# Output projection of a first block as three rounded products of high and low parts, with the loads of two expert halves moved

## The chip, the core and the metric

The kernel runs on one core of one Trainium2 chip. The metric is the time of one execution in device microseconds (us). Engines are named as in the profile: PE (TensorE, matrix products), PEld (its weight loads), DVE (VectorE), ACT (ScalarE), POOL (GpSimd) and SP (SyncE, which only issues loads here). PSUM is the memory that PE writes, in eight banks; the rest of the data lies in SBUF.

## What is computed

Two transformer blocks follow each other on 256 tokens of 1024 features. The change lies in the first, at the last line of its mixer and just ahead of its experts:

```python
def hybrid_mixer(h, ...):
    ...                                   # projections, mLSTM in 4 heads -> y_m, trailing means -> y_p
    return jnp.concatenate([y_m, y_p], axis=-1) @ w_out      # (256 x 1024) @ (1024 x 1024)

def first_block(x, ...):
    h = rmsnorm(x, norm1_g[l])
    x = x + hybrid_mixer(h, ...)
    h = rmsnorm(x, norm2_g[l])
    x = x + moe_ffn(h, ...)               # 32 experts, the best 4 of each token, three 1024 x 1024 matrices each
    return rmsnorm(x, normf_g)
```

The first 512 features of `y` are the heads' (`y_m`), the last 512 the pooled groups' (`y_p`). All is in float32. The second block, with two attention branches and a feed-forward part, comes behind and isn't touched.

## The kernel before

**Phases.** `phase_a` computes the first mixer, its normalisation and the router; `phase_b` runs the 32 experts one after the other; `phase_c`, `phase_e` and `phase_d` are the second block. Each engine has its own program in each phase, written out in order, and semaphores connect them. Nothing is reordered by a scheduler.

**Two ways to multiply.** PE can take float32 operands as they are, or as a rounded type (float32r). For the projections of the first mixer (`Splits`) the weights come in units of 128 by 1024. ACT copies a unit into the rounded type (the high part, L263), and DVE or POOL subtracts that from the original (the low part, L266). A unit is multiplied in three passes: high by high, activation's low by weight's high, activation's high by weight's low (L1142 to L1149 and L1164 to L1171). There are three buffers each for high and low parts, `high_first` and `low_first`; unit u lies in buffer u modulo 3. The high and low parts of the activations are `hTh_first` and `hTl_first`. The last four units, 16 to 19, are those of the output gate.

**The output projection** takes float32 as it is. PE runs `pooled_half(n, t)` (L1239) for column half n and row half t over the four pooled feature chunks, and after the transposes of the gated heads (L1251) it adds the four chunks of the heads (L1263). There are 32 products of 128 by 512; the trace has two records for each. `yT` holds the transposed activations, in the first half of `spare[0]`.

**What PE waits for there.** POOL computes the trailing means in a chain (L889 to L893), and PE multiplies them by `pool_w` (L1226) into two banks. ACT scales them into `yT` (L821). DVE meanwhile divides numerators by denominators (L1000 to L1010), normalises and gates the heads (L1020, L1024), and evicts their transposes (L1028). After the last product of each half DVE adds it to `x` (L1038), ACT squares, and the normalisation goes on row half by row half.

**Loads.** w_out lies in two pieces of `ring25`, OUT0 and OUT1. An expert has six halves of 2 MB: half n of all is number n mod 6 of expert n div 6, in the order gate, gate, up, up, down, down. Eleven are loaded in `phase_a`: 0 to 7 into the eight regular places, and 47, 71 and 95 (`Pieces.LATE`) into `spare[0]`, `spare[1]` and `last_spare`. The rest follow in `phase_b`, each as soon as PE has used the half whose place it takes (L604). `spare[1]` shares memory with `hTh_first`, `last_spare` with `high_first` and `low_first`. The three tables of biases (`btab`, L766) must be there before expert 0 begins. SP issues all of these in a fixed order and stands at each wait.

## Time and profile before

| | us |
|---|---|
| median of 3 runs | 1648.52 (1648.29 to 1649.60) |
| the profiled execution | 1648.02 |
| its span on the core | 1646.3 |
| PE busy | 1624.4 (99%) |
| DVE, ACT, POOL busy | 613.7, 475.8, 302.4 |
| PE waits for POOL's trailing means, ahead of 82.46 | 1.38 |
| output projection on PE, float32 products | 84.58 to 113.2 |
| expert 0 begins | 129.66 |
| experts end | 1036 |

All times in the text are counted from the start of the span. A row of a timeline may merge several like instructions, whose number stands behind the x; its duration then runs from the first start to the last end. Matrix products overlap a little, so the distance of two starts is the better measure of their cost than their length. In brackets stands the idle time of the engine ahead of the row and what ended it.

### The profile page before, as it was taken

To read this page: it belongs to the slowest core of one execution; us is meant where nothing else is said; L and a number is where in the kernel's file an instruction comes from. 1 tells how busy PE (TensorE), PEld (TensorE's weight loads), DVE (VectorE), ACT (ScalarE), POOL (GpSimd) and SP (SyncE) were. 2 spreads that over 40 slices of the span, in tenths; PEclk is the share of its full clock that TensorE was granted. 3 is DMA by queue.
4 is the path that set the end of the run, shared out by engine and by line. 5 is a ranking of instruction groups with operands and counts; after the bars stand their busy time and mean duration, and the time that the engine had idled before them with its cause. 6 is when DMAs were issued, how large, how long until landed. Compare 5 with 4: busy or idle time off the path is not lost. (4 is left out here: it accounts for less than half of the span.)

```text
span 1646.3 us, 22758 instructions
## 1 busy us (share of the span) xinstructions
PE 1624.4 (99%) x9272; PEld 946.4 (57%) x9272; DVE 613.7 (37%) x1144; ACT 475.8 (29%) x695; POOL 302.4 (18%) x192
## 2 busy tenths in 40 slices
PE   9999999999999999999999999999999999999998
PEld 8843333333333333333333333698998999999986
DVE  7743212112121212121121211675485244468852
ACT  5421110111111111111011111574555454454443
POOL 3500000000000000000000000535333624445552
PEclk9999999999999999999999999999999999999999
DMA  9698999999999999999999999353133215456552
GB/s 350 221 367 338 428 427 426 428 427 426 428 426 427 429 426 427 426 428 428 428 428 428 428 428 422 125 179 128 53 123 134 103 52 195 166 166 203 167 192 102
DMA packets 92919, 507.67 MB, mean 308 GB/s; under 512 B 8987, under 2 KB 32584, under 8 KB 68264
## 3 DMA queue, kind: packets, MB, share of 16 engines
q1 hardware_dynamic: 92696, 506.00, 76.1%
q8 instruction: 61, 1.00, 0.3%
q10 hardware_dynamic: 144, 0.52, 0.1%
q14 instruction: 18, 0.15, 0.0%
HBM read 505.46 MB, written 1.05 MB: 308 GB/s over the span
## 5 line engine op out<-in xcount | busy, mean ns | idle before, releaser
L186 POOL TENSOR_TENSOR low<-ring,high 128x1024 fp32r<-128x1024 f32 x81 | 199.6, 2465 | 1262.8 <-ACT high L183 1262.7
L1593 PE MATMUL ps<-ring,x 128*64 128x512 f32 x1536 | 337.5, 594 | 1.8 <-DMA ring<-in_w_up 1.8
L1593 PEld LDWEIGHTS ps<-ring,x 128*64 128x64 f32 x1536 | 108.0, 137 | 227.5 <-issue 222.4
L183 ACT CAST high<-ring 128x1024 fp32r<-128x1024 f32 x162 | 168.2, 1047 | 201.4 <-PE ps L1727 125.5
L1720 PE MATMUL ps<-hTh,high 128*128 128x256 f32 x800 | 198.8, 285 | 2.4 <-DVE hTl L633 1.9
L1721 PE MATMUL ps<-hTl,high 128*128 128x256 f32 x800 | 197.6, 284 | 0.0
L1626 PE MATMUL ps<-ring,x 128*64 128x512 f32 x752 | 171.7, 598 | 0.0
L186 DVE TENSOR_TENSOR low<-ring,high 128x1024 fp32r<-128x1024 f32 x81 | 111.1, 1371 | 146.7 <-ACT high L183 146.6
L1720 PEld LDWEIGHTS ps<-hTh,high 128*128 128x128 f32 x800 | 153.9, 192 | 4.2 <-issue 3.8
L1721 PEld LDWEIGHTS ps<-hTl,high 128*128 128x128 f32 x800 | 154.0, 192 | 0.0
L1466 DVE TENSOR_SCALAR hT<-ps 128x512 f32<-128x512 f32 x32 | 22.1, 692 | 295.8 <-PE ps L1593 295.8
L1593 PE MATMUL ps<-extra,x 128*64 128x512 f32 x512 | 113.8, 594 | 0.0
L1727 PE MATMUL ps<-hTh,low 128*128 128x256 f32 x784 | 110.8, 284 | 0.0
L1626 PEld LDWEIGHTS ps<-ring,x 128*64 128x64 f32 x752 | 49.8, 136 | 103.9 <-issue 103.9
L1727 PEld LDWEIGHTS ps<-hTh,low 128*128 128x128 f32 x784 | 101.9, 193 | 0.0
L1418 DVE TENSOR_TENSOR x<-ps,g 128x512 f32<-128x512 f32 x33 | 22.8, 692 | 204.3 <-PE ps L1559 204.3
L1531 ACT COPY hT<-ps 128x512 f32<-128x512 f32 x32 | 18.8, 586 | 261.5 <-PE ps L1626 261.5
L1526 ACT COPY gpickT<-ps 128x256 f32<-128x256 f32 x32 | 11.9, 372 | 251.5 <-PE ps L1606 251.5
L1522 ACT ACTIVATE hT<-hT 128x512 f32<-128x512 f32 x32 | 20.1, 630 | 220.9 <-DVE hT L1466 220.9
L1472 DVE TENSOR_SCALAR hT<-ps 128x512 f32<-128x512 f32 x32 | 22.1, 691 | 155.5 <-PE ps L1593 155.5
L1593 PEld LDWEIGHTS ps<-extra,x 128*64 128x64 f32 x512 | 36.0, 137 | 75.1 <-issue 74.4
L1568 PE MATMUL ps<-hT,gpickT 64*128 64x512 f32 x264 | 65.6, 615 | 0.7 <-ACT hT L1531 0.7
(465 smaller groups left out, 2181.7 us busy)
## 6 DMA issues: line engine op xcount, KB each, us to landing
ring<-in_w_down SPq DMA_DIRECT2D x52, 2048.0 KB, 20.5
ring<-in_w_gate SPq DMA_DIRECT2D x48, 2048.0 KB, 18.2
ring<-in_w_up SPq DMA_DIRECT2D x48, 2048.0 KB, 18.5
ring<-in_w_in SPq DMA_DIRECT2D x23, 2048.0 KB, 8.2
extra<-in_w_gate SPq DMA_DIRECT2D x16, 2048.0 KB, 18.9
extra<-in_w_up SPq DMA_DIRECT2D x16, 2048.0 KB, 17.5
extra<-in_w_down SPq DMA_DIRECT2D x14, 2048.0 KB, 21.0
ring<-in_w_up SPq DMA_DIRECT2D x22, 1024.0 KB, 7.4
```

The source lines that it names most:

```text
L183: eng.copy(hi, self.raw(u)).then_inc(self.sem("high_split"), 1)
L186: eng.tensor_tensor(lo, self.raw(u), hi.bitcast(F32), ALU.subtract).then_inc(self.sem(who + "_split"), 1)
L1418: bank_free(v.tensor_tensor(xg[:, :, :, :], bank.rearrange("p (c h j) -> p c h j", c=4, h=2), gains, ALU.mult), G_)
L1466: bank_free(v.tensor_scalar(gt[:, :], bank, 7.0, None, ALU.min), GATE)
L1472: bank_free(v.tensor_scalar(up[:, :], bank, 7.0, -7.0, ALU.min, ALU.max), UP)
L1522: act.activation(sg[:, :], gt[:, :], ACT.Sigmoid, scale=1.702).then_inc(sem("sig"), 1)
L1568: last = pe.matmul(total(t, h), gpickT[h * CAP:(h + 1) * CAP, t, :], y[h * CAP:(h + 1) * CAP, :], start=False, stop=final)
L1593: last = pe.matmul(bank[h * CAP:(h + 1) * CAP, :], xg[:, c, kh, :], w[:, c, h * 512:(h + 1) * 512], start=False, stop=kh == 1 and c == 3)
L1626: last = pe.matmul(bank[h * CAP:(h + 1) * CAP, :], aT[:, c, kh, :], w[:, c, h * 512:(h + 1) * 512], start=False, stop=kh == 1 and c == 3)
L1720: pe.matmul(out, wh[:, w], xh[:, c, :], start=c == 0, stop=False)
L1721: last = pe.matmul(out, wh[:, w], xl[:, c, :], start=False, stop=False)
L1727: last = pe.matmul(out, wl[:, c * P:(c + 1) * P], xh[:, c, :], start=False, stop=c == KC - 1)
```

## The change

The output projection takes the three-pass form. w_out is cut into eight pairs (n, q): column half n, and quarter q of the features, two chunks each. Quarters 0 and 1 belong to the heads, 2 and 3 to the pooled groups. High and low parts of a pair lie in buffers that the projections used:

```diff
+    def out_pair(n, q):
+        two = lambda tile: tile.rearrange("p (c n) -> p c n", c=2)
+        flat = lambda tile: two(tile.rearrange("p c n -> p (c n)"))
+        if (n, q) == (0, 2):
+            return flat(hTl[:, 0:4, :]), flat(hTl[:, 4:8, :])
+        if (n, q) == (1, 1):
+            return flat(yTh[:, 4:8, :]), flat(yTl[:, 4:8, :])
+        b = {(0, 3): 2, (1, 2): 0, (1, 3): 1, (0, 0): 2, (0, 1): 0, (1, 0): 1}[n, q]
+        return two(splits.high[:, b, :]), two(splits.low[:, b, :])
```

`y` itself gets a high part `yTh`, in the memory of `hTh_first`, and a low part `yTl_first`, which shares memory with `hT`. ACT makes high parts, the others low ones:

```diff
@@ scalar @@
             splits.ahead(act, "high", 20)
+            act.wait_ge(sem("unit_used"), splits.unnamed(17))
+            out_high(act, 0, 3)
+            act.wait_ge(sem("unit_used"), splits.unnamed(18))
+            out_high(act, 1, 2)
...
+            out_high(act, 0, 2)
+            out_high(act, 1, 3)
+            for j in range(2):
+                y_high(2 + j, ("pool", j), P1["pool_scale"] + 2 * j)
...
+            out_pair_used(act, 0)
+            out_high(act, 0, 0)
+            out_pair_used(act, 1)
+            out_high(act, 0, 1)
+            for j in range(2):
+                y_high(j, ("ym", j), P1["head_norm_g"] + 2 * j)
+            out_high(act, 1, 0)
+            out_high(act, 1, 1)
@@ gpsimd, behind the trailing means @@
+            for n, q in ((0, 2), (1, 3), (0, 0), (0, 1), (1, 0)):
+                out_low(g, n, q)
@@ vector @@
             splits.ahead(v, "low0", 20)
+            out_low(v, 0, 3)
+            out_low(v, 1, 2)
...
+            for j in range(2):
+                y_low(2 + j, ("pool", j), P1["pool_scale"] + 2 * j)
             v.wait_ge(sem("hroot"), 1)
...
+                y_low(j, ("ym", j), P1["head_norm_g"] + 2 * j)
+            out_low(v, 1, 1)
```

`out_high` waits for the piece and casts; `out_low` waits for the high part and subtracts; `out_pair_used(act, i)` waits until PE has ended pooled group i. `y_high` is two scaled evictions of a bank, `y_low` two fused multiply-and-subtract operations on the same bank. On PE the pooled part is one group for each column half, and both stand ahead of the transposes:

```diff
-            pooled_half(0, 0)
-            pooled_half(0, 1)
-            pooled_half(1, 0)
+            pooled_half(0, (3, 2))
+            pooled_half(1, (2, 3))
             pe.wait_ge(sem("ym"), NT)
...
-            pooled_half(1, 1)
```

SP's order of loads, with the waits:

```diff
-            for n, use in (..., (3, ("o", 1)), (Pieces.LATE[2], ("o", 1)), (Pieces.LATE[1], ("pool", 1)),
-                           (6, ("ym", 1)), (7, ("ym", 1)), (4, ("out", 0, 1)), (5, ("out", 1, 1)), (Pieces.LATE[0], ("out", 1, 1))):
-                banks.done(sp, use)
+            for n, use in (..., (3, ("o", 1)), (Pieces.LATE[0], ("pool", 1)),
+                           (6, ("ym", 1)), (7, ("ym", 1)), (4, None), (5, None), (Pieces.LATE[1], ("out", 1, 1)),
+                           (Pieces.LATE[2], ("out", 1, 1))):
+                if use is not None:
+                    banks.done(sp, use)
+                else:
+                    sp.wait_ge(sem("low0_split"), LOW0_UNITS + (1 if n == 4 else 3))
+                    sp.wait_ge(sem("low1_split"), LOW1_UNITS + (4 if n == 4 else 5))
```

The bias tables stay tied to half 95 and move with it. The scrap output of the squares goes to `xn` instead of `hT`, and the bank of ("out", 1, 1) is the one that the warming products ("lg") use later.

**DVE ahead of the numerators**, before and then now. `low_first` is written by the low parts of the last units; in the new rows L738 is `out_low`.

```order
L990 TENSOR_TENSOR extra<-ps,extra 128x128
L266 TENSOR_TENSOR low_first<-ring25,high_first 128x1024 [waits high_split] x5
L1000 SCALAR_TENSOR_TENSOR den<-ps,ccol 128x2 [waits bankA_full0]
L1001 TENSOR_TENSOR den<-ps,den 128x2 [waits dveA]
L1002 RECIPROCAL den<-den 128x2 [waits dveA]
```

```order
L1046 TENSOR_TENSOR extra<-ps,extra 128x128
L268 TENSOR_TENSOR low_first<-ring25,high_first 128x1024 [waits high_split] x5
L738 TENSOR_TENSOR low_first<-ring25,high_first 128x1024 [waits high_split] x2
L1070 SCALAR_TENSOR_TENSOR den<-ps,ccol 128x2 [waits bankA_full0]
L1071 TENSOR_TENSOR den<-ps,den 128x2 [waits dveA]
L1072 RECIPROCAL den<-den 128x2 [waits dveA]
```

Two subtractions of 128 by 1024 have come in ahead of the first numerator.

**ACT from the last unit's high part on**, before and then now. L815 and L857 are the output gate's sigmoid, L821 and L863 the scaled evictions, L732 is `out_high`.

```order
L263 CAST high_first<-ring25 128x1024 [waits ringA_loaded3,unit_used]
L815 ACT_TABLE_LOAD
L815 ACTIVATE extra<-ps 128x512 [waits bankA_full6]
L815 ACTIVATE extra<-ps 128x512 [waits bankA_full7]
L821 ACTIVATE spare<-ps,prm1 128x256 [waits bankA_full4]
L821 ACTIVATE spare<-ps,prm1 128x256
L821 ACTIVATE spare<-ps,prm1 128x256 [waits bankA_full5]
L821 ACTIVATE spare<-ps,prm1 128x256
```

```order
L863 ACTIVATE hTh_first<-ps,prm1 128x256 [waits bankA_full5]
L863 ACTIVATE hTh_first<-ps,prm1 128x256
L438 ACT_TABLE_LOAD
L438 ACTIVATE stat<-ones 128x1
L873 ACTIVATE rs<-rs 128x8 [waits hvar]
L732 CAST high_first<-ring25 128x1024 [waits ringA_loaded4,unit_used] x2
L863 ACTIVATE hTh_first<-ps,prm1 128x256 [waits bankA_full2]
L863 ACTIVATE hTh_first<-ps,prm1 128x256
L863 ACTIVATE hTh_first<-ps,prm1 128x256 [waits bankA_full3]
L863 ACTIVATE hTh_first<-ps,prm1 128x256
L732 CAST high_first<-ring25 128x1024 [waits ringA_loaded5]
L732 CAST hTh_first<-ring25 128x1024 [waits ringA_loaded5]
```

The casts of (0,0) and (0,1) wait for PE's groups (`unit_used`) and stand ahead of the evictions of the transposed heads; two more follow them.

**PE from the transposes to the end of the projection**, before and then now (of the last section the first row half's first rows).

```order
L1251 MATMUL ps<-ident,extra 128x128 x3
L1251 MATMUL ps<-ident,extra 128x128 [waits bankA_free2]
L1251 MATMUL ps<-ident,extra 128x128 x3
L1239 MATMUL ps<-ring25,spare 128x512 [waits bankA_free3,ringA_loaded5]
L1239 MATMUL ps<-ring25,spare 128x512 x3
L1257 MATMUL ps<-ident,prow2 128x113 [waits bankA_free4,prow2_in]
L1263 MATMUL ps<-ring25,spare 128x512 [waits bankA_free2,bankA_free1]
L1263 MATMUL ps<-ring25,spare 128x512 x15
```

```order
L1336 MATMUL ps<-ident,extra 128x128 x3
L1341 MATMUL ps<-ident,prow2 128x113 [waits bankA_free4,prow2_in]
L1357 MATMUL ps<-high_first,hTh_first 128x512 [waits high_split]
L1357 MATMUL ps<-high_first,hTh_first 128x512
L1357 MATMUL ps<-low_first,hTh_first 128x512 [waits low1_split]
L1357 MATMUL ps<-low_first,hTh_first 128x512
L1357 MATMUL ps<-high_first,yTl_first 128x512 [waits bankA_free2]
L1357 MATMUL ps<-high_first,yTl_first 128x512
L1357 MATMUL ps<-high_first,hTh_first 128x512 [waits high_split]
L1357 MATMUL ps<-high_first,hTh_first 128x512
L1357 MATMUL ps<-low_first,hTh_first 128x512 [waits low1_split]
L1357 MATMUL ps<-low_first,hTh_first 128x512
```

The pooled product between the transposes and the last section has gone ahead of them, and each pair of products in the first row half now waits for its own part.

**SP's loads around the projection**, before and then now. L604 and L607 are expert halves.

```order
L604 DMA ring25<-in_w_up 128x4096 [waits bankA_full7]
L766 DMA btab<-in_b_gate 32x1024 [waits bankA_full7]
L766 DMA btab<-in_b_up 32x1024
L766 DMA btab<-in_b_down 32x1024
L604 DMA last_spare<-in_w_down 128x4096
L604 DMA spare<-in_w_down 128x4096 [waits bankA_full5]
L604 DMA extra<-in_w_gate 128x4096 [waits bankA_full2] x2
L604 DMA ring25<-in_w_down 128x4096 [waits bankA_full7]
L604 DMA ring25<-in_w_down 128x4096 [waits bankA_full3]
L604 DMA spare<-in_w_down 128x4096 [waits bankA_full3]
```

```order
L607 DMA ring25<-in_w_up 128x4096 [waits bankA_full7]
L607 DMA spare<-in_w_down 128x4096 [waits bankA_full5]
L607 DMA extra<-in_w_gate 128x4096 [waits bankA_full3] x2
L607 DMA ring25<-in_w_down 128x4096 [waits low1_split,low0_split] x2
L607 DMA spare<-in_w_down 128x4096 [waits bankA_full1]
L804 DMA btab<-in_b_gate 32x1024 [waits bankA_full1]
L804 DMA btab<-in_b_up 32x1024
L804 DMA btab<-in_b_down 32x1024
L607 DMA last_spare<-in_w_down 128x4096
```

Halves 4 and 5 now wait for the splits, and the bias tables stand behind ten halves instead of four.

## Rows read from the trace of the kernel before

**Rows 1.** The page: busy time with share of span; busy tenths of the DMA in 40 slices.

```profile
PE 1624.4 (99%) x9272; PEld 946.4 (57%) x9272; DVE 613.7 (37%) x1144; ACT 475.8 (29%) x695; POOL 302.4 (18%) x192
...
DMA  9698999999999999999999999353133215456552
```

**Rows 2.** Windows, expert stage: stretch, its length, engines' busy us, PEclk, DMA share, GB/s.

```profile
206.00:300.00 94.00, 94.00 (x450) 30.51 (x446) 18.73 (x38) 11.43 (x18) 0.00 (x0) 1.00 1.01 427
```

**Rows 3.** Timeline of PE, last experts: start, us, engine, line, operation, count, idle before.

```profile
989.64 3.65 PE L1593 MATMUL ps<-ring,x 128*64 128x512 f32 x16 [0.89 <-DMA ring<-in_w_up]
...
1019.05 3.65 PE L1593 MATMUL ps<-ring,x 128*64 128x512 f32 x16 [0.94 <-DMA ring<-in_w_up]
```

**Rows 4.** Timeline of PE, last projection to expert 0.

```profile
72.71 0.39 PE L1164 MATMUL ps<-high_first,hTh_first 128*128 128x512 f32 x1
...
75.47 0.39 PE L1164 MATMUL ps<-high_first,hTh_first 128*128 128x512 f32 x1
...
82.46 1.97 PE L1226 MATMUL ps<-extra,spare 128*128 128x256 f32 x8 [1.38 <-issue]
84.58 10.54 PE L1239 MATMUL ps<-ring,spare 128*128 128x512 f32 x24 [0.16 <-ACT spare L821]
94.96 1.04 PE L1251 MATMUL ps<-ident,extra 128*128 128x128 f32 x8
95.83 3.60 PE L1239 MATMUL ps<-ring,spare 128*128 128x512 f32 x8
...
99.37 13.91 PE L1263 MATMUL ps<-ring,spare 128*128 128x512 f32 x32
...
129.66 1.09 PE L1585 MATMUL ps<-btab,hot 32*64 32x512 f32 x8
```

**Rows 5.** Timelines of POOL and then DVE, pooling chain; single operations.

```profile
69.92 1.19 POOL L890 COPY extra<-spare 128x4 f32<-128x4 f32 x1
...
72.87 2.32 POOL L889 TENSOR_TENSOR extra<-extra 128x762 f32<-128x762 f32 x1
75.14 0.18 POOL L890 COPY extra<-extra 128x6 f32<-128x6 f32 x1
...
80.02 2.35 POOL L893 TENSOR_TENSOR extra<-extra,spare 128x1024 f32<-128x1024 f32 x1
...
70.98 1.21 DVE L266 TENSOR_TENSOR low_first<-ring,high_first 128x1024 fp32r<-128x1024 f32 x1
...
72.12 1.76 DVE L266 TENSOR_TENSOR low_first<-ring,high_first 128x1024 fp32r<-128x1024 f32 x1
...
78.89 0.16 DVE L1000 SCALAR_TENSOR_TENSOR den<-ps,ccol 128x2 f32<-128x2 f32 x1 [5.01 <-PE ps L1218]
```

**Rows 6.** Timeline of ACT: a high part, and the eviction of the pooled groups.

```profile
70.14 1.05 ACT L263 CAST high_first<-ring 128x1024 fp32r<-128x1024 f32 x1 [0.29 <-PE ps L1171]
...
83.60 1.70 ACT L821 ACTIVATE spare<-ps,prm 128x256 f32<-128x256 f32 x4 [4.54 <-PE ps L1226]
```

**Rows 7.** Timeline of SP, issues of loads.

```profile
79.75 0.74 SPq L766 DMA_DIRECT2D btab<-in_b_down  x1
...
134.37 3.76 SPq L604 DMA_DIRECT2D ring<-in_w_up  x2
```

**Rows 8.** DMA issues in 95 to 96.4 and 78.2 to 81: count, size, us to landing.

```profile
extra<-in_w_gate SPq DMA_DIRECT2D x1, 2048.0 KB, 7.8
...
last_spare<-in_w_down SPq DMA_DIRECT2D x1, 2048.0 KB, 12.6
...
btab<-in_b_down SPq DMA_DIRECT2D x1, 128.0 KB, 8.6
```

**Rows 9.** Window ahead of and behind the start of expert 0.

```profile
125.00:135.00 10.00, 8.56 (x44) 2.98 (x44) 5.78 (x33) 1.87 (x2) 0.00 (x0) 1.00 0.28 111
```

**Rows 10.** Window in the second block.

```profile
1245.00:1248.00 3.00, 3.00 (x17) 3.00 (x16) 2.00 (x5) 2.99 (x8) 0.00 (x0) 0.54 1.05 407
```

**Rows 11.** Waits of PE: us in total, times, longest.

```profile
PE ps L2326 <- ACT egb L1903: 1.6, 1, 1.6
```

More of the change, by code:

```diff
@@ L684, in phase_a @@
     inv = part(1, 8 * S, 4, S)
-    uT = yT[:, 0:4, :]
+    uT = part(0, 0, 4, S, of=spare)
     DT = part(0, 8 * S, NT, NH, S)
@@ L709, in phase_a, with out_raw, out_pair_used, out_high @@
     splits = env["splits"]
+    def out_pair(n, q):
[7 more added lines that the diff above has]
+        return two(splits.high[:, b, :]), two(splits.low[:, b, :])
+    def out_raw(n, q):
+        return piece(OUT0 + n)[:, 2 * q:2 * q + 2, :]
+    def out_pair_used(eng, i):
+        eng.wait_ge(sem("unit_used"), splits.unnamed(len(splits.units) - 1) + i + 1)
+    def out_high(act, n, q):
+        ring.landed(act, OUT0 + n)
+        splits.made("high", ("out", n, q), act.copy(out_pair(n, q)[0], out_raw(n, q)))
+    def out_low(eng, n, q):
+        who = "low0" if (n, q) in Splits.OUT_LOW0 else "low1"
+        hi, lo = out_pair(n, q)
+        splits.wait(eng, "high", ("out", n, q))
+        splits.made(who, ("out", n, q), eng.tensor_tensor(lo, out_raw(n, q), hi.bitcast(F32), ALU.subtract))
+    LOW0_UNITS = 4 + 20 - len(Splits.BY_ONE)
+    LOW1_UNITS = len(Splits.BY_ONE)
     for g, name in ((Q_, "qk"), (K_, "qk"), (V_, "v"), (U_, "u"), (O_, "o")):
@@ L816, in _, with y_high @@
                 banks.release(last, ("o", t))
-            for g in range(4):
-                if g % 2 == 0:
-                    bank = banks.take(act, ("pool", g // 2))
-                last = act.activation(yT[:, 4 + g, :], bank[:, (g % 2) * S:(g % 2 + 1) * S], ACT.Copy,
-                                      scale=prm1[:, P1["pool_scale"] + g:P1["pool_scale"] + g + 1])
-                if g % 2:
-                    banks.release(last, ("pool", g // 2))
+            def y_high(j, key, scale):
+                bank = banks.take(act, key)
+                for i in range(2):
+                    last = act.activation(yTh[:, 2 * j + i, :], bank[:, i * S:(i + 1) * S], ACT.Copy,
+                                          scale=prm1[:, scale + i:scale + i + 1])
+                splits.made("high", ("y", j), last)
+            out_high(act, 0, 2)
+            out_high(act, 1, 3)
+            for j in range(2):
+                y_high(2 + j, ("pool", j), P1["pool_scale"] + 2 * j)
             k.prepare(act)
@@ L992, in _, with y_low @@
             splits.ahead(v, "low0", 20)
+            out_low(v, 0, 3)
+            out_low(v, 1, 2)
+            def y_low(j, key, scale):
+                bank = banks.take(v, key)
+                splits.wait(v, "high", ("y", j))
+                for i in range(2):
+                    c = 2 * j + i
+                    last = v.scalar_tensor_tensor(yTl[:, c, :], bank[:, i * S:(i + 1) * S], prm1[:, scale + i:scale + i + 1],
+                                                  yTh[:, c, :].bitcast(F32), ALU.mult, ALU.subtract)
+                    if i == 0:
+                        chain.mark(last)
+                    else:
+                        banks.release(last, key)
             for j in range(NT):
```

68 lines of the change are left out of this document (46 added, 22 removed).

## The prediction

> **What bounds the kernel now.** I read the busy times and the forty slices first [rows 1]: TensorE (PE) works for 99% of the span, and from 165 to 1029 us (the fifth slice to the 25th) the DMA slices are full too. So two things can set the end. The window of one stretch of the expert stage [rows 2] shows both full at once: PE 94.00 us of 94.00 at the full clock, DMA share 1.01, 427 GB/s. The reader is to ask which is ahead. The last two experts tell it [rows 3]: PE waits 0.89 and 0.94 us there for a half of w_up to land, and these are its only waits for the DMA. The loads thus fall behind PE by a little with each expert and catch it just at the end. They are issued as PE frees a buffer, so their chain starts with expert 0, by the issue at 134.37 [rows 7]. If expert 0 starts earlier or later, both chains move together, unless a load finds the queue full. Everything behind the experts follows in time. So the question is one number: by how much does expert 0, at 129.66 [rows 4], move?
>
> Before it PE is nearly without a gap. The one of size is 1.38 us ahead of 82.46, where PE waits until GpSimd (POOL) has finished its pooling chain: its last step ends at 80.02 + 2.35 = 82.37 [rows 4, 5].
>
> **The product itself.** Now 32 products of 128 by 512 in plain float32 take 10.54 + 3.60 + 13.91 us [rows 4], 28.05 in all; the 64 records are two for each product, so one is 0.877. The new form takes three rounded products for each. Its price stands in the rows of the projections, which are written in the same form: 12 products from 72.71 to 75.47 [rows 4], 0.230 each, so three cost 0.69. 96 times 0.230 is 22.1 us. On PE alone 5.9 us go away. What remains of that depends on who delivers the parts.
>
> **POOL's chain, which PE waits for.** Two subtractions for low parts, pairs (0,3) and (1,2), come to VectorE (DVE) before its numerator loop. They cost DVE nothing, which idles 5.01 us ahead of 78.89 [rows 5]. They lie, though, beside POOL's chain. ScalarE (ACT) can make the high parts once units 17 and 18 are used, at 72.7 and 75.5, plus 0.2 for the hand-over and 1.05 for the cast [rows 6]; DVE gets them at 74.0 and 76.75. The rows show what such a subtraction does to POOL: a copy of 4 elements takes 1.19 us under one and 0.18 without, and the DVE op itself is 1.21 when it comes first and 1.76 when a POOL op was running; it begins, in effect, when that POOL op ends [rows 5]. So one holds back the other for a whole instruction. Played through: the first waits for the op of 762 elements to end at 75.19 and holds POOL to 76.35, 1.1 us; the second runs 77.2 to 78.4 and costs another 1.05. POOL's chain ends 2.15 us later, at 84.5, and PE's gap grows from 1.38 to 3.5 us. Bounds: 0, if the subtractions fall between POOL's ops; 2.4, two whole DVE ops. I take 2.15.
>
> The Trainium skill (SBUF — State Buffer, Who interferes with whom) says that a DVE instruction with two inputs in SBUF and a GpSimd instruction that reads SBUF exclude each other for the whole instruction, and do not share. It speaks against this change. By it the delay is as above; if they shared, it would be near the lower bound, and the whole result 2 us better.
>
> **The start of the product.** Now PE starts after the first pair of pooled groups is evicted. The new order starts with quarter 3, the second pair: 83.60 + 1.70 = 85.30 [rows 6] instead of 84.58 [rows 4], plus 0.15: 0.87 us later. With POOL's 2.15 and rounding the first product stands at 87.55. Two groups of 24 at 0.230 follow without a stall: the high parts of (0,2), (1,3) are made before the pool banks are full; the low parts (0,2), (1,3) follow POOL's chain at 2.4 us each, ready at 87.0 and 89.5, needed at 88.5 and 96; DVE's low parts of y are ready by 88.3, needed at 91.2. PE ends them at 98.6. DVE has the gated heads by 93, so the transposes start at once and take 0.87 [rows 4]; the second bank is full at 99.7.
>
> **The last section, where cover is gone.** Before, a pooled product of 3.60 us lay between the transposes and the last section [rows 4] and hid the eviction. It is moved ahead, and more now hangs on the eviction. On ACT's queue: cast (0,1), only after the second group (its buffer), 98.8 to 99.85; two evictions in high form, 0.85 each by [rows 6], to 100.7 and 101.55; casts (1,0) and (1,1) to 102.5 and 103.5. POOL: low (0,1) 99.9 to 102.3, low (1,0) 102.55 to 104.95. DVE: low parts of y to 101.6 and 102.4, then low (1,1), which waits for POOL's op: 104.9 to 106.1. PE in its order: it waits from 99.6 to 100.8 for y's high part (1.2), runs to 104.0, waits for low (1,0) until 105.05 (1.05), passes (1,1) at 106.45, ends the first row half at 107.35, and the second, 24 products, at 112.9. Before, this was 113.2 (99.37 + 13.91, less the overlap of the last). Sum: -5.9 + 2.15 + 0.87 + 1.2 + 1.05 + 0.3 of hand-overs = **-0.3 us**. The bounds: -2.5 with POOL undelayed, +1.5 with every hand-over on POOL and ACT 0.5 us longer. Behind it nothing changes; the normalisation's chain hangs on the last bank as before, and the block of three warming products waits for another bank that is free 0.9 us later, inside a wait that is there.
>
> **The loads.** The order on SP is new: the halves 6 and 7 after the transposes (99.7), 4 and 5 when the splits have read w_out (102.4, 106.2), 71, the table of biases and 95 after the last product (113). A first half lands 7.8 us after its issue [rows 8], each next one 2.1 MB / 427 GB/s = 4.9 us later [rows 2]: 107.5, 112.4, 117.3, 122.2, 127.1. The biases add 1.6 at most: their three issues, the last at 79.75 and landed 8.6 us later [rows 7, 8], followed a half on the queue in the same way, so 128.7; expert 0 now needs them at 129.4. Then 95 at 133.6. In the present trace the queue is busy for 28% from 125 to 135 [rows 9], so the extra halves fill idle time, and the load at 134 finds the queue free again by about 1.5 us. Price: 0. If the cover fails, the price is what expert 0 waits. Memory places are otherwise the same, and the squares' scrap output into another tile costs the same.
>
> **The rivals.** (a) The clock. PE's gap of 3.5 us, with another of 1 us close behind, is longer than any wait of PE in the present trace, the longest being 1.6 [rows 11]. The only fall in mid-run shows the price: the granted clock is 0.54 (near the level of 1.2 GHz) from 1245 to 1248, though PE was busy for all of that window [rows 10]. So a gap isn't the only cause, and 3 us at half rate cost some 1.7: 1649.9. The Trainium skill (TensorE: Matmul & The Clock Gate, Why this matters for your kernels) has the clock fall when PE idles between bursts, which speaks for it; no row here tests it. (b) Faster: POOL isn't held, and the waits of the last section vanish, because the hand-overs overlap better than played through. Then -5.9 + 0.87 + 0.6 of waits = -4.4, 1644.1, if the biases also land earlier; were they the limit, it would be -3.1. Against it are [rows 5]. (c) Slower: the biases. If they don't land before 95 but with it, at 133.6, expert 0 waits from 129.4: 4.0 us, 1652.2. It decides from a landing after 129.4 on, and the margin is 0.7 us. Against it: with a half of w_down queued behind them they landed well before it: 8.6 us after 79.75, which is 88.4, against 12.6 us after an issue that followed at once, 93.1 [rows 7, 8]. (d) That the change doesn't do what it says: the order on PE, ahead of this text, shows the three passes, so I give it no chance.
>
> **How the numbers follow.** The profiled execution is 1648.02 us, 0.50 under the median 1648.52 of the three runs. -0.3 gives 1647.7 there, **1648.2** against the median. Chances: forecast 0.64, (a) 0.12, (b) 0.11, (c) 0.13. A measurement here tells about 0.2%, 3.3 us, from no change. The forecast and (a) lie within: 0.76; faster 0.11; slower 0.13. The forecast's own range is 1646.0 to 1650.0. With (a), most of (c) and the edge of (b) it is 1645.2 to 1652.2.
>
> **What would show it.** Right: POOL's last pooling step ends near 84.5; PE's gap before the pool products is 3 to 4 us; waits of about 1 us each for y's high part and for POOL's low part (1,0); the last product ends near 113, expert 0 starts near 129.4, its biases landing just before. Wrong: a gap under 2 us (the hold isn't there); a granted clock near half between 84 and 100 (a); a wait of PE before expert 0 (c); or waits for the DMA in the last experts that differ from 1.8 us in sum by more than 1, which would mean that loads and PE don't move together.

## The result: slower by 0.35%, and the profile after

The changed kernel takes 1653.39 us, the median of six runs (1652.47 to 1656.95), beside 1648.28 us for the kernel before in its six: a ratio of 1.0035, with an interval of 1.0022 to 1.0048 (it goes by the means; after's is 1654.3). That is 5.1 us more, against 0.3 us less in my forecast, and above the end of my range, 1652.2.

The profiled execution after has a span of 1651.2 us against 1646.3, so it shows the whole loss, 4.9 us. The first view is the page's, its span and its busy times; they answer to [rows 1] and give no hint, since PE works 1.0 us less and still has 98% of a longer span:

```profile
span 1651.2 us, 22863 instructions
PE 1623.4 (98%) x9304; PEld 952.1 (58%) x9304; DVE 621.7 (38%) x1153; ACT 485.1 (29%) x707; POOL 317.3 (19%) x197
```

The loss is found by laying the starts on PE beside those of [rows 4]. The timeline of PE after (start, us, line, operation, tiles, shapes, count, idle before it and what ended it), from the pool products to the second expert's bias product:

```profile
84.37 3.31 PE L1296 MATMUL ps<-extra,spare 128*128 128x256 f32 x8 [3.23 <-issue]
88.70 1.17 PE L1323 MATMUL ps<-high_first,hTh_first 128*128 128x512 f32 x4 [1.02 <-ACT hTh_first L863]
...
94.36 2.01 PE L1323 MATMUL ps<-high_first,hTh_first 128*128 128x512 f32 x8
...
99.90 1.03 PE L1336 MATMUL ps<-ident,extra 128*128 128x128 f32 x8
...
102.02 0.70 PE L1357 MATMUL ps<-high_first,hTh_first 128*128 128x512 f32 x2 [0.99 <-ACT hTh_first L863]
...
106.07 0.74 PE L1357 MATMUL ps<-low_first,hTh_first 128*128 128x512 f32 x2 [0.56 <-POOL low_first L738]
...
114.07 1.04 PE L524 MATMUL ps<-ident,xn 128*128 128x128 f32 x8
...
130.07 0.63 PE L1654 MATMUL ps<-ident,x 128*128 128x128 f32 x4 [1.33 <-ACT x L1609]
132.33 1.76 PE L1680 MATMUL ps<-btab,hot 32*64 32x512 f32 x8 [1.63 <-DMA btab<-in_b_down]
134.02 16.62 PE L1688 MATMUL ps<-ring,x 128*64 128x512 f32 x64
...
163.93 1.09 PE L1680 MATMUL ps<-btab,hot 32*64 32x512 f32 x8
```

and two rows of the same view of before, which [rows 4] lacks: the transposes behind the last product, and the second expert's bias product.

```profile
113.11 1.04 PE L521 MATMUL ps<-ident,xn 128*128 128x128 f32 x8
...
157.91 1.09 PE L1585 MATMUL ps<-btab,hot 32*64 32x512 f32 x8
```

The product's part of the loss is small: these transposes start at 114.07 instead of 113.11, +0.96. The start of expert 0 has moved from 129.66 to 132.33, +2.67: there is a second wait, of 1.63 us, for the last table of biases. And by the second expert, at 163.93 instead of 157.91, it is +6.02: expert 0 takes 31.60 us where it took 28.25. Nothing is given back by the loads: PE's waits for the DMA in the last experts are 0.92 and 0.94 us, against 0.89 and 0.94 in [rows 3].

Why expert 0 is longer stands in the windows. The three stretches of after (length, busy us of each engine, granted clock, share of the DMA, GB/s):

```profile
84.80:88.20 3.40, 2.88 (x8) 1.72 (x6) 2.58 (x14) 1.32 (x4) 3.40 (x2) 0.50 0.09 39
132.60:139.40 6.80, 6.80 (x22) 1.68 (x16) 2.85 (x12) 0.00 (x0) 0.00 (x0) 0.50 0.51 207
1245.00:1248.00 3.00, 3.00 (x10) 1.44 (x9) 0.00 (x0) 2.68 (x3) 1.57 (x1) 1.00 0.01 4
```

The clock column reads 0.50, the level of 1.2 GHz, for 3.4 us behind the pause at 81.1 to 84.4 and for 6.8 us behind the pauses at 128.7 to 132.3. At either place before has 1.00. In [rows 10] the reader saw a fall of the same kind in before, at 1245; after has none there, and gets 1.6 us back.

Two more views say who was late. The timeline of POOL ahead of 84.3, which answers to [rows 5]:

```profile
72.94 2.32 POOL L943 TENSOR_TENSOR extra<-extra 128x762 f32<-128x762 f32 x1
75.20 1.18 POOL L944 COPY extra<-extra 128x6 f32<-128x6 f32 x1
...
81.93 2.34 POOL L947 TENSOR_TENSOR extra<-extra,spare 128x1024 f32<-128x1024 f32 x1
```

and that of DVE in the same time:

```profile
74.05 2.28 DVE L738 TENSOR_TENSOR low_first<-ring,high_first 128x1024 fp32r<-128x1024 f32 x1
76.82 1.47 DVE L738 TENSOR_TENSOR low_first<-ring,high_first 128x1024 fp32r<-128x1024 f32 x1 [0.48 <-ACT high_first L732]
```

The subtractions on DVE (L738) stand at 74.05 and 76.82, as played through. The copy of 6 elements takes 1.18 us, not 0.18 [rows 5]. The chain ends at 81.93 + 2.34 = 84.27, 1.90 us later than in [rows 5]; 0.06 of it were there before the subtractions began, so they hold it by 1.84.

The issues of DMAs after, each for the short stretch of one issue (size, us to landing), which answer to [rows 8]: the halves 6 and 7, issued at 100.96 and 101.33, number 5 at 107.12, 71 at 114.26, and the last biases at 115.57:

```profile
extra<-in_w_gate SPq DMA_DIRECT2D x1, 2048.0 KB, 7.6
...
extra<-in_w_gate SPq DMA_DIRECT2D x1, 2048.0 KB, 13.2
...
ring<-in_w_down SPq DMA_DIRECT2D x1, 2048.0 KB, 17.2
...
spare<-in_w_down SPq DMA_DIRECT2D x1, 2048.0 KB, 16.4
...
btab<-in_b_down SPq DMA_DIRECT2D x1, 128.0 KB, 16.7
```

They land at 108.6, 114.5, 124.3, 130.7 and 132.3. In the windows across that time the queue is full throughout, but moves less where the biases are in it:

```profile
121.00:125.00 4.00, 4.00 (x15) 1.97 (x14) 3.05 (x19) 1.57 (x5) 0.00 (x0) 1.00 1.01 430
128.00:131.00 3.00, 1.37 (x8) 0.42 (x4) 0.83 (x8) 1.18 (x2) 0.00 (x0) 1.00 1.03 273
```

### The profile page after: what moved, and what is told of

The parts are those of the page before. It is cut to its first block and busy times, and to the rows that moved or that the text cites. A ratio compares the mean times of both kernels' runs of the same rounds, so it can differ in the third digit from the quotient of the medians.

```text
span 1651.2 us, 22863 instructions
## 1 busy us (share of the span) xinstructions
PE 1623.4 (98%) x9304; PEld 952.1 (58%) x9304; DVE 621.7 (38%) x1153; ACT 485.1 (29%) x707; POOL 317.3 (19%) x197
## 3 DMA queue, kind: packets, MB, share of 16 engines
HBM read 505.46 MB, written 1.05 MB: 307 GB/s over the span
## 5 line engine op out<-in xcount | busy, mean ns | idle before, releaser
L1688 PEld LDWEIGHTS ps<-ring,x 128*64 128x64 f32 x1536 | 108.6, 138 | 230.3 <-issue 225.7
```

Of the source, the lines that this page charges most:

```text
L1688: last = pe.matmul(bank[h * CAP:(h + 1) * CAP, :], xg[:, c, kh, :], w[:, c, h * 512:(h + 1) * 512], start=False, stop=kh == 1 and c == 3)
```

## Experiments

All kernels below ran in rounds with the kernel before, whose medians were 1648.1 to 1648.3; the changed kernel's 1653.4 is that of its own six runs. A change of 0.1% is 1.6 us, and the intervals are about 0.001 to either side.

The first four take the two suspects apart, the order of the biases' loads and the two subtractions beside POOL.

**The biases first.** The biases are issued ahead of the half 71 instead of behind it; nothing else changes.

```diff
-                if n == Pieces.LATE[2]:
+                if n == Pieces.LATE[1]:
                     for m, name in enumerate(("b_gate", "b_up", "b_down")):
```

> The changed kernel, but SP issues the three tables of biases ahead of half 71 and not behind it. Nothing is left out. Theory: PE's wait of 1.63 us for the biases before expert 0 makes the pause long enough for the clock to fall, and the fall (6.8 us at half rate, from 132.6) costs another 3.3. Then both go away: expert 0 starts at about 130.7, its gate and up products take 13.95 us again and not 16.62, and the time is 1653.4 - 4.9 = 1648.5. Rival: the clock falls there for another reason (the router's small products ahead of it); then only the wait goes, 1651.8. Second rival: the halves queued late delay the biases wherever they stand; then nothing changes, 1653.4.

Measured: 1652.06 us (1647.24 to 1653.72), ratio 1.0017 [1.0007, 1.0026], where I expected 1648.5: a miss, close to the first rival's 1651.8. In the profile the last table lands 12.2 us after its issue at 117.52, at 129.7, and the wait for it is gone; only the pause for ACT stands ahead of expert 0, in the timeline of PE:

```profile
132.53 0.63 PE L1654 MATMUL ps<-ident,x 128*128 128x128 f32 x4 [1.36 <-ACT x L1609]
133.09 1.09 PE L1680 MATMUL ps<-btab,hot 32*64 32x512 f32 x8
```

The window behind that place:

```profile
134.00:138.00 4.00, 4.00 (x16) 1.15 (x14) 2.86 (x12) 0.12 (x1) 0.00 (x0) 0.57 0.95 397
```

The clock is at 0.57 all the same: a stretch at half clock was there behind the pause of 1.36 us alone. So the wait's 1.6 us can be taken away by the order, but with it the clock isn't always restored. The first pause has 6.8 us at half clock behind it here, twice that of the changed kernel. The runs spread over 6.5 us, more than those of any other kernel.

**The low parts on POOL.** The subtractions (0,3) and (1,2) go from DVE to POOL, behind its chain, and SP's waits for the halves 4 and 5 follow them there (those lines aren't shown); the biases stay last.

```diff
-    OUT_LOW0 = ((0, 3), (1, 2), (1, 1))
+    OUT_LOW0 = ((1, 1),)
...
-            for n, q in ((0, 2), (1, 3), (0, 0), (0, 1), (1, 0)):
+            for n, q in ((0, 3), (0, 2), (1, 2), (1, 3), (0, 0), (0, 1), (1, 0)):
...
-            out_low(v, 0, 3)
-            out_low(v, 1, 2)
```

> The changed kernel, but the low parts of the pairs (0,3) and (1,2) are made by POOL behind its pooling chain and not by DVE beside it. Nothing is left out. Theory: the two DVE subtractions hold POOL's chain by 1.9 us, and the longer pause of PE lets the clock fall from 84.8 to 88.2, which costs 1.3. Then POOL's chain ends near 82.4, PE's gap is 1.4 and not 3.2, the first product starts near 85.5 and not at 88.70, and all behind it moves 3.2 us ahead, the biases too, so that the wait and the fall at expert 0 stay: 1650.2. Rival: the clock falls there anyway, because of the small products of the numerators; then 1651.5. Rival: POOL is now too slow with seven low parts and PE waits for them; then the gain is eaten, 1652 or more.

Measured: 1650.56 us (1648.88 to 1652.93), ratio 1.0013 [1.0004, 1.0023], against 1650.2 expected. The hold is gone in the timeline of PE: the pause ahead of the pool products is 1.40 us and they take 1.97, at full clock. The wait for the biases remains:

```profile
83.61 1.97 PE L1295 MATMUL ps<-extra,spare 128*128 128x256 f32 x8 [1.40 <-issue]
...
130.77 1.22 PE L1679 MATMUL ps<-btab,hot 32*64 32x512 f32 x8 [2.15 <-DMA btab<-in_b_down]
```

The window behind that wait has 3.4 us at 0.50:

```profile
131.60:135.00 3.40, 3.40 (x12) 1.00 (x10) 1.59 (x8) 0.00 (x0) 0.00 (x0) 0.50 0.76 310
```

All of this is shifted by 1.1 us, since this execution has a stretch at half clock near 43 us too, with no pause ahead of it. Others have it as well (table below), and it is part of no suspect.

**Both.** The two edits above together.

> Both edits together: the biases ahead of half 71, and all pooled pairs' low parts on POOL. Nothing is left out. Theory: the parts add, 1653.4 - 4.9 - 3.2 = 1645.3, the clock is at full rate from 10 us to at least 1200 us, and PE's waits are 1.4 ahead of the pool products, 1.0 for the high part of y, and none for the biases. Rival: the loads are the bound, since half 8 can't start before half 95 is through; then expert 0 starts early but PE waits more for w_up in the last experts, and the time stays above 1647.

Measured: 1645.69 us (1644.63 to 1648.05), ratio 0.9987 [0.9978, 0.9997]: faster than the kernel before, by 0.13%, less than the 0.2% that I had called a measurable change, but with an interval that leaves out 1. The timeline of PE:

```profile
82.47 1.97 PE L1295 MATMUL ps<-extra,spare 128*128 128x256 f32 x8 [1.39 <-issue]
85.45 1.17 PE L1322 MATMUL ps<-high_first,hTh_first 128*128 128x512 f32 x4 [1.02 <-ACT hTh_first L864]
...
110.77 1.04 PE L524 MATMUL ps<-ident,xn 128*128 128x128 f32 x8
...
127.34 1.09 PE L1679 MATMUL ps<-btab,hot 32*64 32x512 f32 x8
...
155.59 1.09 PE L1679 MATMUL ps<-btab,hot 32*64 32x512 f32 x8
```

One window from the projections to past the start of expert 1:

```profile
20.00:162.00 142.00, 135.53 (x768) 95.29 (x768) 90.72 (x217) 56.98 (x82) 45.52 (x27) 1.00 0.84 323
```

The chain on POOL ends at 82.37, as in [rows 5]; the first product starts at 85.45, 0.87 us behind [rows 4], which is my term for the other order of the pairs, 0.87; the transposes behind the last product at 110.77, 2.34 us earlier than before; expert 0 at 127.34 takes 28.25 us. The clock stays at 1.00 for the whole stretch. I had expected 1645.3.

**The subtractions in the kernel before.** Two unused subtractions of the same shape at the same place of DVE's queue, and no other change: the disputed hold by itself.

```diff
             splits.ahead(v, "low0", 20)
+            for i in range(2):
+                v.tensor_tensor(hT[:, 4 * i:4 * i + 4, :].rearrange("p c s -> p (c s)"), x[:, 0, :], x[:, 1, :], ALU.subtract)
```

> The kernel before, with two subtractions of 128 by 1024 on DVE ahead of its numerators, both inputs in SBUF, whose result nobody uses. Nothing else differs, nothing is left out. Theory: they hold POOL's chain by 2 us, PE's gap grows from 1.4 to 3.4 us, the granted clock falls for about 3.4 us behind it, and the products start some 3 us later: 1651.3. Rival: POOL is held but the clock doesn't fall: 1650.4. Rival: no hold, 1648.3.

Measured: 1650.96 us (1649.68 to 1652.73), ratio 1.0016 [1.0006, 1.0025], against 1651.3 expected. The timeline of PE:

```profile
84.64 3.01 PE L1228 MATMUL ps<-extra,spare 128*128 128x256 f32 x8 [3.21 <-issue]
87.44 11.15 PE L1241 MATMUL ps<-ring,spare 128*128 128x512 f32 x24
...
116.59 1.04 PE L521 MATMUL ps<-ident,xn 128*128 128x128 f32 x8
```

The window behind the pause:

```profile
85.40:88.80 3.40, 3.40 (x8) 2.28 (x7) 1.22 (x11) 1.93 (x5) 0.00 (x0) 0.50 1.05 317
```

POOL's chain ends 2.17 us later, of which 0.35 were there when it began, so the subtractions hold it by 1.82. PE's pause is 3.21 us instead of 1.38, and the stretch at half clock is there as in the changed kernel, with the product in plain float32. The transposes behind the last product start at 116.59, 3.48 us later than before: 0.35 from ahead of the chain, 1.83 of pause and 1.30 of half clock, since from the pool products to these transposes it takes 31.95 us and not 30.65.

The next four ask what the clock is worth, and test the loads alone. The unused products are of 128 by 256, some 0.5 us each, like those that the kernel has at other places; nothing reads them.

**The first pause filled.** After's kernel with five unused products ahead of the pool products.

```diff
             pe.wait_ge(sem("pool_w_in"), 16)
+            keep_busy(pe, banks.claim(pe, ("pool", 0)), ones, 5)
             pe.wait_ge(sem("pooled"), 1)
```

> The changed kernel with five unused products of 128 by 256 (0.56 us each in the profile after) on TensorE in the pause ahead of the pool products, where it waits 3.23 us for GpSimd. GpSimd's hold stays. If the half-clock stretch at 84.8 us comes from the pause, it is gone (1.7 us) and the first pool products take 1.97 us, not 3.31; the second pause, for the biases ahead of expert 0, and its 6.8 us of half clock stay: 1653.4 - 1.7 = 1651.7. If the stretch doesn't come from the pause, it is there still and the time stays at 1653.4.

Measured: 1651.55 us (1649.03 to 1653.90), ratio 1.0016 [1.0007, 1.0025]; 1.8 us below the changed kernel, 1.7 expected (its profiled execution, 1652.1 us, is no guide to that, since it has stretches near 43 and at 1251 that after's has not). The timeline of PE:

```profile
82.39 2.32 PE L308 MATMUL ps<-ones 128*128 128x256 f32 x10
85.74 1.99 PE L1297 MATMUL ps<-extra,spare 128*128 128x256 f32 x8 [1.02 <-POOL extra L947]
...
132.41 1.99 PE L1681 MATMUL ps<-btab,hot 32*64 32x512 f32 x8 [1.62 <-DMA btab<-in_b_down]
```

The pool products take 1.99 us and not 3.31: the stretch is gone, while POOL is held as before. The biases are waited for as in the changed kernel (1.62 us), and the 6.8 us at half clock around that are there, with 1.99 us for their products, which take 1.09 at full clock [rows 4]:

```profile
131.40:138.20 6.80, 5.79 (x18) 1.55 (x20) 4.06 (x17) 0.34 (x1) 0.00 (x0) 0.50 0.71 287
```

**The loads alone.** The kernel before, in which only the biases and the half behind them are issued last.

```diff
-            for n, use in ((0, ("qk", 3)), (1, ("v", 1)), (2, ("u", 1)), (3, ("o", 1)), (Pieces.LATE[2], ("o", 1)), (Pieces.LATE[1], ("pool", 1)),
-                           (6, ("ym", 1)), (7, ("ym", 1)), (4, ("out", 0, 1)), (5, ("out", 1, 1)), (Pieces.LATE[0], ("out", 1, 1))):
+            for n, use in ((0, ("qk", 3)), (1, ("v", 1)), (2, ("u", 1)), (3, ("o", 1)), (Pieces.LATE[1], ("pool", 1)),
+                           (6, ("ym", 1)), (7, ("ym", 1)), (4, ("out", 0, 1)), (5, ("out", 1, 1)), (Pieces.LATE[0], ("out", 1, 1)),
+                           (Pieces.LATE[2], ("out", 1, 1))):
```

> The kernel before, with its product in plain float32, in which only the table of biases and the one half of w_down behind it are issued last, after the other halves, as in the changed kernel. Theory: the biases land 1 to 2 us after 129.7, TensorE waits so long ahead of expert 0, close behind its pause of 1.33 us, and the clock is at half for 3.4 us or more behind it: 1648.3 + 1.5 + 1.7 = 1651.5. Rival, in which only long pauses such as the 3.23 us lower the clock: the wait alone, 1649.8. Rival, in which the biases' place matters only with the new order of halves 4 and 5: no wait, 1648.3.

Measured: 1651.19 us (1649.45 to 1653.77), ratio 1.0017 [1.0008, 1.0027], against 1651.5 expected. The last table lands at 132.9, and PE waits for it behind the pause for ACT (timeline of PE):

```profile
130.50 0.63 PE L1560 MATMUL ps<-ident,x 128*128 128x128 f32 x4 [1.33 <-ACT x L1515]
132.93 1.09 PE L1586 MATMUL ps<-btab,hot 32*64 32x512 f32 x8 [1.80 <-DMA btab<-in_b_down]
```

The window behind the start of expert 0:

```profile
134.00:137.40 3.40, 3.40 (x12) 0.95 (x12) 1.57 (x7) 0.00 (x0) 0.00 (x0) 0.50 0.71 294
```

So the late biases cost some 3 us in a kernel whose product is untouched, the wait and one stretch of 3.4 us at half clock.

**Both pauses filled.** After's kernel with five unused products ahead of the pool products, and two and three around the transposes ahead of expert 0.

```diff
+            keep_busy(pe, bank_claim(pe, DOWN, 0), ones, 2)
             turned(0)
+            keep_busy(pe, bank_claim(pe, DOWN, 0), ones, 3)
             pe.wait_ge(sem("btab_in"), 48)
```

> The changed kernel with unused products in both pauses: five ahead of the pool products, and two and three around the transposes ahead of expert 0, where TensorE waits 1.33 us for ScalarE and 1.63 us for the biases. Nothing that others wait for comes earlier by it. Theory: the half-clock stretches at 84.8 and 132.6 us are gone, 1.7 + 3.4 us: 1653.4 - 5.1 = 1648.3, expert 0 still starts near 130.6 and waits for the biases. Rival, in which the waits themselves are the price: 1653.4 to 1652.5.

Measured: 1649.88 us (1648.54 to 1650.95), ratio 1.0011 [1.0001, 1.0020]; 3.5 us below the changed kernel, where I expected 5.1. The loads and POOL are as late as in the changed kernel (expert 0 starts at 132.71), but the clock is full from 80 to 162 us, and expert 1 starts at 160.96, after 28.25 us. The window over both places:

```profile
80.00:162.00 82.00, 75.80 (x375) 43.32 (x373) 39.42 (x139) 22.79 (x45) 17.05 (x12) 1.00 0.85 336
```

In the profiles expert 1 comes 2.97 us earlier than in the changed kernel. It is the 3.35 us of half clock in expert 0, less 0.38 by which the biases land later. The first stretch's 1.3 us don't show in this execution, because a stretch near 42 us pushed POOL's chain 1.3 us later, to 85.55, and with it all that follows. Whether the missing 1.6 us of the median are the same, one traced execution can't say.

**The faster kernel filled.** The kernel with both edits, two unused products in each of its two pauses.

```diff
+            keep_busy(pe, banks.claim(pe, ("pool", 0)), ones, 2)
             pe.wait_ge(sem("pooled"), 1)
...
+            keep_busy(pe, bank_claim(pe, DOWN, 0), ones, 2)
             turned(0)
```

> The kernel with the low parts (0,3) and (1,2) on GpSimd and the biases first (1645.7 in its own run), with two unused products ahead of the pool products and two ahead of the transposes before expert 0 (pauses of 1.39 and 1.33 us). Its profile had no half clock before 1105 us. Theory: nothing is left there to gain in the profiled execution, and the spread of its runs (1644.6 to 1648.1) narrows towards its lower end: 1645.0 to 1645.7. Rival: the falls that occur are elsewhere, and the spread stays.

Measured: 1646.38 us (1645.23 to 1647.90), ratio 0.9988 [0.9979, 0.9997], where I expected 1645.0 to 1645.7: no better than without. Its profile has a stretch at half clock near 43 and one at 1245, as the rival has it. But the filling also has a price of its own. The two products ahead of the transposes begin only after a pause of 1.22 us, hardly shorter than the 1.33 without them, and then stand in the way: from the transposes behind the last product to expert 0 it takes 17.39 us (112.25 to 129.64), and 16.57 without them (110.77 to 127.34). These 0.8 us are as much as the difference of the two medians, 0.7. The kernel with both edits and without filling stays the lowest.

The last two check the sum from its ends.

**The biases first, both pauses filled.** Of the suspects only the hold on POOL is left. The edits are those above: the one line of the biases, five products ahead of the pool products, two ahead of `turned(0)`.

> The changed kernel with the biases issued ahead of the last two halves, and unused products in the pauses: five ahead of the pool products, two ahead of the transposes before expert 0. Only the subtractions' hold on GpSimd is left of the suspected costs. Theory: against the kernel with both pauses filled (1649.9) the wait for the biases, some 1.6 us, goes and nothing else: 1648.3, equal to the kernel before; expert 0 takes 28.25 us. Rival, in which GpSimd's hold costs about 1.9 us more than my sum for the product: 1650.2.

Measured: 1648.72 us (1648.20 to 1649.92), ratio 1.0004 [0.9994, 1.0014]. That is my forecast's case, a product that gains what the hold takes, with no wait for the biases and no fall of the clock behind the pauses, and it comes out within 0.2% of before. It is near my 1648.2, though 0.8 us of it come from the two products ahead of expert 0, which delay it as in the kernel above. It also has the narrowest spread of the experiments. The timeline of PE, with these two products (L308) at 130.03:

```profile
85.77 1.99 PE L1297 MATMUL ps<-extra,spare 128*128 128x256 f32 x8 [1.02 <-POOL extra L947]
...
114.13 1.04 PE L524 MATMUL ps<-ident,xn 128*128 128x128 f32 x8
...
130.03 1.12 PE L308 MATMUL ps<-ones 128*128 128x256 f32 x4 [1.22 <-PEq L760]
```

The clock is full up to expert 1 in the window:

```profile
80.00:162.00 82.00, 75.84 (x375) 42.92 (x375) 39.42 (x139) 23.91 (x46) 17.22 (x12) 1.00 0.86 342
```

**The two subtractions in the kernel before, with the pause filled.** Again both edits as above, the loop of two subtractions and the line with five unused products.

> The kernel before with the two unused subtractions on VectorE beside GpSimd's pooling chain (1651.0 in its own run) and five unused products of 128 by 256 on TensorE in the pause that they make. Theory: the hold stays (the chain ends 2.0 us later, the product starts 1.5 to 2 us later) and the stretch at half clock behind it, worth 1.65 us in the profile, goes: 1648.3 + 1.9 = 1650.2 or less. Rival, in which the fall isn't caused by the pause: 1651.0 and a stretch near 85 us.

Measured: 1652.52 us (1648.81 to 1653.90), ratio 1.0023 [1.0013, 1.0033]: a miss, it should have been at or below 1650.2 and is 1.6 us above the kernel without the filling (1.0 by the means, 1651.9 and 1650.9, which the spread of the runs doesn't set apart). The windows at the filled pause and behind the start of expert 0:

```profile
85.40:88.80 3.40, 2.86 (x10) 1.93 (x11) 2.25 (x16) 1.81 (x5) 0.32 (x1) 1.00 1.08 341
134.60:138.00 3.40, 3.40 (x12) 0.96 (x10) 2.19 (x10) 0.00 (x0) 0.00 (x0) 0.50 0.01 4
```

The stretch near 85 is gone as expected (1.00): five products in the pause take it away, with POOL's hold still there. But now one stands behind the pause of 1.33 us ahead of expert 0, where the kernel without filling had none.

The profiles side by side; "behind the start" is the stretch at half clock in the first us of expert 0:

| kernel | half clock near 85 | wait for biases | behind the start | expert 0 | elsewhere (start of stretch) |
|---|---|---|---|---|---|
| before | 0 | 0 | 0 | 28.25 | 1245 |
| after | 3.4 | 1.63 | 6.8 | 31.60 | none |
| biases first | 6.8 | 0 | 3.4 | 29.93 | 42, 1250 |
| low parts on POOL | 0 | 2.15 | 3.4 | 29.89 | 43, 1248 |
| both | 0 | 0 | 0 | 28.25 | 1105 |
| before, two subtractions | 3.4 | 0 | 0 | 28.25 | 1249 |
| after, first pause filled | 0 | 1.62 | 6.8 | 31.06 | 43, 1251 |
| before, biases late | 0 | 1.80 | 3.4 | 29.93 | 42, 1250 |
| after, both filled | 0 | 0.4 | 0 | 28.25 | 42, 1110 |
| both, filled | 0 | 0 | 0 | 28.25 | 43, 1245 |
| biases first, both filled | 0 | 0 | 0 | 28.25 | 43 |
| before, two subtractions, filled | 0 | 0 | 3.4 | 29.94 | 42, 1070, 1114 |

A stretch of 3.4 us within expert 0 costs 1.64 to 1.69 us, 6.8 us cost 3.35 (2.81 where the stretch begins a little ahead of it). Ahead of the pool products the clock fell behind all three pauses of 3.2 us left open, behind none of the four that five products filled, and behind none of the four pauses of 1.4 us left open. All three kernels with unused products at both places have no fall at expert 0, and all four with a wait for the biases left open have 3.4 or 6.8 us of it.

With the pause of 1.33 to 1.36 us for ACT alone it is open: two profiles have a fall there and three have none. These two belong to the eight with a stretch near 42, the three to the four without. The two groups differ from the first microseconds on: the clock rises to full at 4.3 to 5.6 us in the eight and at 6.2 to 6.9 us in the four, and the twelve warming products at the start take 7.0 to 7.6 us and 7.9 to 8.3. So the fall ahead of expert 0 in the last kernel goes with the execution that was traced, and isn't shown to come from the filling at the other place.

How often a kernel's clock falls, its runs tell: each has a mean granted clock, which a stretch of 3.4 us lowers by 0.001. In the changed kernel it is 0.995 to 0.996 in the four runs of 1652.5 to 1653.8 us and 0.993 in the two of 1656.6 and 1657.0. With the biases first it is 0.997 at 1647.2 and 1648.7 us, and 0.994 or 0.995 in the six from 1651.4 us up; with the pauses filled too it is never under 0.997. The last kernel has 0.999 in its runs of 1648.8 and 1650.1 us, at or under the 1650.2 that I expected, and 0.995 to 0.997 in the seven from 1651.2 up. The spread is thus in the clock. At which place it fell in a run isn't known, and what brings the stretch near 42 and the late ones isn't either.

## Why the prediction was wrong, point by point

**The product and its helpers: right.** My sum up to the end of the product was -0.3 us without the clock. The kernel with the biases first and both pauses filled has the changed product at full clock: from the pool products to the transposes behind the last product it takes 28.36 us (85.77 to 114.13), and the kernel before 30.65 (82.46 to 113.11). The product is thus worth -2.29 us, and my terms for it, -5.9 + 0.87 + 1.2 + 1.05 + 0.3, make -2.48. The 0.231 us for a product in the second group (24 from 94.36 to 99.90) and the 0.87 us for the other order are as I had them. Two terms were off and cancel, which is luck. For the old product I added up 28.05 us of lengths, which overlap; by the starts it is 27.6, the new one is 22.3, and PE is rid of 5.2 us and not 5.9. And the waits were smaller than played through, 0.99 for 1.2 and 0.56 for 1.05.

**The hold on POOL: right in kind, a little large.** 2.15 us were taken, 1.84 measured in the changed kernel and 1.82 in the kernel before with two subtractions. The Trainium skill (SBUF — State Buffer, Who interferes with whom) has a DVE instruction with two inputs in SBUF contend with a GpSimd instruction that reads SBUF, and calls the lock on the port pair that they share exclusive. The copy of 1.18 us against 0.18 agrees, and with the low parts behind POOL's own chain nothing is held.

**The clock: wrong, the chance and the size.** I put the fall behind the long pause at 0.12, as rival (a), because the only fall in the profile, [rows 10], came while PE was busy, and took that as evidence that pauses matter little. It showed only that a pause isn't needed. The fall did come: 3.4 us at 0.50 from 84.8 us. Its price was 1.34 us, since from the pool products to the transposes it takes 29.70 us (84.37 to 114.07) and 28.36 at full clock, where the rival had 1.7. That figure didn't follow from its row either: 3 us at half rate cost 1.5. The runs show that the pause made the fall: it came with the same pause in the kernel before, and went in all four kernels in which the pause was filled. The Trainium skill (TensorE: Matmul & The Clock Gate, Why this matters for your kernels) has it that gaps between bursts of products let the clock fall; here the trace agrees for the pause of 3.2 us, and shows falls behind shorter ones too. And the rival stopped at one place. The start of expert 0 already had a pause of 1.33 us. With a second one beside it the clock fell there for 6.8 us, 3.35 us of time. This second fall is the largest single part of the loss, and my sum had no term for it. My rival (c) priced a late table of biases by the wait alone.

**The loads: wrong in one step, "so 128.7".** The last table landed at 132.3, 3.6 us later than my figure, which had 0.7 us to spare. The parts: the halves were issued 1.26 us later than I had them (100.96 for 99.7), since PE was late; the second half came 5.97 us after the first and not 4.9; and from number 5 to the last table it took 7.95 us where I had 4.9 + 1.6. In the last part the price of the biases is the term that was mis-sized. I had allowed 1.6 at most. But the window 128:131 shows the DMA engines fully busy at 273 GB/s, against 430 at 121:125: the small transfers take time of the engines beyond their bytes, 1.1 us in those 3 us alone. In the trace's packets, those of a table (4 KB) take 0.29 us each in that window, and those of the halves (16 KB) 0.90 us beside them, against 0.61 at 121:125. So half and tables took 3.1 us more than the half's own 4.9, which is the measure of the term that I had at 1.6. The 7.8 (7.6 measured) and the 4.9 between halves in a full queue (114.5, 119.4, 124.3) were right. So was the argument against rival (c), that the tables land well before the half issued behind them: 95 landed at 137.9. It didn't look at the half ahead of them: the first two tables landed before 71 (at 129.3 and 129.9 for 130.7), but the third, for which PE waits, didn't.

**The sum.** From before to after, at expert 1: 1.91 us for the later pool products (1.84 of hold), 1.34 at half clock, -2.29 for the product and what surrounds it, 1.71 for the biases, 3.35 at half clock in expert 0: 6.02 us. From there to the last expert it grows by some 0.5 us, not explained, and the absent fall at 1245 gives 1.6 back: 4.9. The half clock is thus 4.7 of the 6.0 us at expert 1, the biases' wait 1.7, and the product with its hold -0.4. Two steps failed. The sum had no term for the clock: it priced pauses by their own length and carried "behind it nothing changes" past a place that already had a pause, where the runs show 1.34 and 3.35 us at half clock. And "Price: 0" for the loads rested on 1.6 us for the tables of biases, which took 3.1 and landed at 132.3, not 128.7.

**What would show it,** as I had listed, came in three signs: the gap of 3 to 4 us (right), a granted clock near half between 84 and 100 (a), a wait of PE before expert 0 (c). Both rivals occurred, together, (c) with a wait of 1.6 us and not 4.0; I had treated them as exclusive.

## What to carry to other kernels

Price a pause of TensorE twice: by its length, and by the stretch at half clock that may follow, 1.3 to 1.7 us for each 3.4 us here, and look at every place downstream that already has a pause and may get a second one. Where another engine's lateness is unavoidable, a few unused products in the pause gave the second price back (1653.4 to 1649.9 us), though in another kernel there was no gain (1651.0 and 1652.5). See that they run inside the pause: two that began only at its end cost 0.8 us. Put small tables that a stage needs first ahead of the large loads that it needs later, and don't place a subtraction with two inputs on VectorE beside a chain of GpSimd that TensorE waits for: with both mended the same product is faster than plain float32, 1645.7 us against 1648.3.

## What the runs showed of the hardware

- The granted clock fell to 0.50 in stretches of 3.4 or 6.8 us at places where PE had paused for 3.2 us (84.8), for 1.33 and 1.63 us close together (132.6), but also, in some executions, while PE was busy (near 42 and between 1070 and 1251 us).
- Behind a lone pause of 1.33 to 1.36 us ahead of expert 0 the clock fell in two of five executions. The two are those whose clock had risen to full early (4.4 and 4.9 us) and had fallen near 42, the three those in which it rose at 6.2 to 6.9 us and hadn't. Of five executions that isn't more than a hint.
- Three tables of 128 KB, 32 partitions each, held the DMA engines at 273 GB/s with a share of 1.03, where halves of 2 MB run at 430. Their packets of 4 KB took 0.29 us each, those of 16 KB 0.61 us in the halves alone.
- The ten runs of one kernel can spread by 6.5 us (biases first) or by 1.7 (the same with its pauses filled). The slower runs are those with the lower mean clock, 0.994 against 0.997.
